# A gated delta rule on one core: filler products of the scan cut in halves, and each head's decays made one head earlier

## The reference, cut to what matters

```python
proj = h @ in_w                                        # q, k, v, z of every head, and a, b
qkv = silu(causal_dwconv(proj[..., :o1], conv_w))
q = l2norm(q) * (GDN_DK ** -0.5);  k = l2norm(k)
beta = sigmoid(b_in);  g = -exp(a_log) * softplus(a_in + dt_bias)
g = cumsum(g, axis=-1)                                 # inside a chunk
decay_mask = exp(where(causal, g[:, None] - g[None, :], -inf))
a_mat = where(strict, (k_beta @ k.T) * decay_mask, 0)
t_mat = inverse(eye + a_mat)
attn = where(causal, (q @ k.T) * decay_mask, 0)
...
def step(state, inp):                                  # the scan over chunks
    v_new = u_c - w_c @ state
    o_c = q_c @ state + attn_c @ v_new
    state = state * e_c + k_c.T @ v_new
o = rmsnorm(o) * silu(z);  out = o @ out_w
```

## Time and profile before

| what | value |
|---|---|
| median of 3 runs (lowest, highest) | 2101.68 us (2100.63, 2105.51) |
| the profiled execution's own time | 2100.75 us |
| its span, first to last instruction | 2098.8 us |
| PE busy, share of the span | 2047.3 us, 98% |
| DVE, ACT, POOL busy | 1351.1, 630.7, 244.7 us |
| mean granted TensorE clock | 0.997 |
| DeltaNet heads, from the first filler to the last o_flip | 458.4 to 1136.1 us of the span |

### The profile page before, as it was taken

One profiled execution on the slowest core, in us unless ns is written; L12 is line 12 of the kernel. 1 busy time (PEld: TensorE's weight loads), 2 busy tenths in 40 slices (PEclk: granted clock), 3 DMA queues, 4 the chain that ended last, 5 costly groups with the idle time before them and its releaser, 6 DMA issues. The chain is left out here.

```text
span 2098.8 us, 20772 instructions
## 1 busy us (share of the span) xinstructions
PE 2047.3 (98%) x6914; PEld 1044.5 (50%) x6914; DVE 1351.1 (64%) x1900; ACT 630.7 (30%) x1051; POOL 244.7 (12%) x188
## 2 busy tenths in 40 slices
PE   7999999999999999999998999999999999999998
PEld 4444444446566566656454454544444444444443
DVE  3787753266756656666823697439999997434633
ACT  4345531223443443443213410013211112241021
POOL 0000001113213213211102100011000000003200
PEclk9999999999999999999999999999999999999999
DMA  9333389241111211111420316389522222333021
GB/s 349 124 116 112 97 282 237 84 101 38 48 31 36 47 31 36 47 32 35 148 36 20 131 51 113 91 233 250 127 58 78 66 71 65 110 105 130 20 100 60
DMA packets 243824, 207.17 MB, mean 99 GB/s; under 512 B 52204, under 2 KB 202785, under 8 KB 243745
## 3 DMA queue, kind: packets, MB, share of 16 engines
q1 hardware_dynamic: 213393, 157.25, 25.1%
q0 software_dynamic: 13056, 42.99, 8.3%
q10 hardware_dynamic: 17312, 6.10, 1.3%
HBM read 182.55 MB, written 60.33 MB: 116 GB/s over the span
## 5 line engine op out<-in xcount | busy, mean ns | idle before, releaser
L2345 PE MATMUL bank<-hT,ring 128*128 128x512 f32 x576 | 254.2, 592 | 0.0
L2345 PE MATMUL bank<-resid,ring 128*128 128x512 f32 x432 | 191.3, 592 | 0.0
L2345 PEld LDWEIGHTS bank<-hT,ring 128*128 128x128 f32 x576 | 109.4, 190 | 137.8 <-issue 136.6
L1312 PE MATMUL bank<-hT,ring 128*128 128x512 f32 x336 | 157.7, 595 | 1.8 <-ACT silu_z L1549 1.8
L3265 DVE SCALAR_TENSOR_TENSOR yT<-s_arena,yT 128x1024 f32<-128x1024 f32 x120 | 152.8, 1273 | 0.0
L3265 DVE SCALAR_TENSOR_TENSOR s_arena<-s_arena 128x1024 f32<-128x1024 f32 x112 | 142.6, 1273 | 0.0
L2317 PE MATMUL bank<-hT,ring 128*128 128x512 f32 x320 | 139.4, 594 | 0.0
L2345 PEld LDWEIGHTS bank<-resid,ring 128*128 128x128 f32 x432 | 82.1, 190 | 103.3 <-issue 102.6
L2317 PEld LDWEIGHTS bank<-hT,ring 128*128 128x128 f32 x320 | 60.1, 190 | 73.7 <-issue 73.5
L2390 PE MATMUL bank<-ssm_y,ring 128*128 128x512 f32 x192 | 83.4, 592 | 0.0
L1312 PEld LDWEIGHTS bank<-hT,ring 128*128 128x128 f32 x336 | 58.4, 190 | 49.9 <-issue 49.5
(11 more groups left out here) (585 smaller groups left out, 3595.1 us busy)
## 6 DMA issues: line engine op xcount, KB each, us to landing
ada<-in_ada_w SPq DMA_DIRECT2D x8, 2048.0 KB, 8.1
ring<-in_gdn_in_w SPq DMA_DIRECT2D x32, 512.0 KB, 4.1
ring<-in_w_in SPq DMA_DIRECT2D x54, 256.0 KB, 2.9
ab_U_sums<-in_w_in POOLq DMA_DIRECT2D x6, 2048.0 KB, 19.2
resid<-in_x SPq DMA_DIRECT2D x8, 1024.0 KB, 8.8
ring<-in_lru_in_w SPq DMA_DIRECT2D x16, 512.0 KB, 3.9
ring<-ab_U_sums SPq DMA_DIRECT2D x32, 256.0 KB, 2.9
lru_arena<-in_ada_w SPq DMA_DIRECT2D x6, 1024.0 KB, 13.7
```

The costliest lines, as they stand in the source:

```text
L1312: last = nc.tensor.matmul(bank[:, to, :], w[:, k, :], v[:, k, :], start=(first and k == 0), stop=(k == KB - 1), skip_group_check=not only)
L2345: last = nc.tensor.matmul(bank[:, to, :], w[:, k, :], src[:, k, :], start=(start and k == 0), stop=(k == HK - 1), skip_group_check=not alone)
```

## The change

- The fillers from P4a on (the last six products) are cut into two matmuls of 256 columns each, so a filler is half as long there: 32 whole units and 48 halves.
- `fill` now puts 2 units instead of 4 ahead of `k_flip`, 12 instead of 13 behind `kk`, two halves (one unit before) ahead of the first state read, in each chunk two halves behind the read and two behind `new` (one unit each before), and, new, one half ahead of every state read from c=1 on. In the last head that place takes one whole unit. What is left stands behind the scan: 7 halves instead of 4 units, and in the last head 1 unit instead of 8.
- ACT's three copies in the scan move to c=2, c=3 and c=5.
- The decays of head h+1 are made in head h: the subtraction on DVE behind level 16, the mask on POOL behind the sums for half "b", the exponential on ACT at level 32 between `prod32` and `inv32`. Those of head 0 are made ahead of the loop: DVE behind the first convolutions, POOL behind its first weight sums, ACT behind the first silu(z).
- The query norm's root (`q_rms`) moves on ACT from level 32 to behind `prod64`, and its reciprocal on DVE (`q_inv`, `q_dec`) to behind `mem_zero`.

```diff
@@ project_pairs @@
-                        def product(pr, to, w, v, name, first=False, only=False):
-                            w = blocks(pr)[w]
+                        def product(pr, to, w, v, name, first=False, only=False, parts=1):
+                            w, width = blocks(pr)[w], HALF // parts
                             for k in range(KB):
...
+                                for n in range(parts):
+                                    cols_ = slice(n * width, (n + 1) * width)
+                                    last = nc.tensor.matmul(bank[:, to, cols_], w[:, k, :], v[:, k, cols_], start=(first and k == 0 and n == 0),
+                                                            stop=(k == KB - 1), skip_group_check=not only)
...
-                        yield from product("a", 0, "A22", tok_sum4, "P4")
+                        yield from product("a", 0, "A22", tok_sum4, "P4", parts=2)
...
-                        yield from product("b", 2, "S4", tok22, "P3")
+                        yield from product("b", 2, "S4", tok22, "P3", parts=2)
@@ body, tensor @@
-                        fill(4, 0)
+                        fill(2, 0)
...
-                        fill(13, 18)
+                        fill(12, 18)
...
                             if c == 0:
-                                fill(1, 0)
+                                fill(2, 0)
...
                             else:
+                                fill(1, 1)
                                 hd_dve.wait(pe, f"mem{c - 1}", h)
...
-                            fill(1, 2)
+                            fill(2, 2)
@@ body, gpsimd @@
+                    def masked(head):
+
+                        dve_r.wait(g, "rel", head)
+                        pool_r.mark(g.tensor_tensor(decayT[:, :, :], decayT[:, :, :], along(causal[:, :]), ALU.add), "rel")
+
                     def body(h, second, first):
-                        hd_dve.wait(g, "rel", h)
-                        hd_pool.mark(g.tensor_tensor(decayT[:, :, :], decayT[:, :, :], along(causal[:, :]), ALU.add), "rel")
...
                         if second:
                             weight_sums("b", h + 1)
+                            masked(h + 1)
...
                     weight_sums("a", 1)
+                    masked(0)
@@ body, scalar @@
+                    def decays(head):
+
+                        pool_r.wait(act, "rel", head)
+                        act_r.mark(act.activation(decayT[:, :, :], decayT[:, :, :], ACT.Exp), "decay")
...
-                        hd_pool.wait(act, "rel", h)
-                        hd_act.mark(act.activation(decayT[:, :, :], decayT[:, :, :], ACT.Exp), "decay")
...
-                            if s == levels[1]:
+                            if s == levels[1] and after is not None:
+                                decays(after)
+                            if s == levels[2]:
                                 hd_act.mark(act.activation(stat[:, 1, :], stat[:, 1, :], ACT.Sqrt, bias=eps2[:, 1:2], scale=float(P)), "q_rms")
...
-                            if c == 4 and after is not None:
+                            if c == 5 and after is not None:
                                 keep(2, "b", h, "P5", "C22")
...
                     take_z(0)
+                    decays(0)
                     for_heads(act, body)
@@ body, vector @@
+                    def relative(head):
+
+                        dve.wait_ge(g_in, (head + 1) * 16)
+                        dve_r.mark(dve.tensor_tensor(decayT[:, :, :], decayT[:, :, :], per_tok("g", head), ALU.subtract), "rel")
+
+                    relative(0)
...
-                        dve.wait_ge(g_in, (h + 1) * 16)
-                        hd_dve.mark(dve.tensor_tensor(decayT[:, :, :], decayT[:, :, :], per_tok("g", h), ALU.subtract), "rel")
...
+                            if n == 0 and after is not None:
+                                relative(after)
```

More of the change, by code:

```diff
@@ L1085, in block_program @@
                            + [f"vc{j}" for j in range(TAPS4)] + ["q_ss", "v_tok"]
-                           + [n for s in levels for n in halves(f"invT{s}") + (["q_inv", "q_dec"] if s == levels[1] else [])]
-                           + ["mem_zero"] + [f"{n}{c}" for c in range(NCH) for n in ("delta", "mem", "o")]
+                           + [n for s in levels for n in halves(f"invT{s}")]
+                           + ["mem_zero", "q_inv", "q_dec"] + [f"{n}{c}" for c in range(NCH) for n in ("delta", "mem", "o")]
                            + ["o_inv", "o_tok", "y"])
-            hd_pool = Steps(sem("gdn_pool"), ["rel"] + [f"part{s}" for s in levels[:-1]])
+            hd_pool = Steps(sem("gdn_pool"), [f"part{s}" for s in levels[:-1]])
+            dve_r, pool_r, act_r = Steps(sem("gdn_rel_dve"), ["rel"]), Steps(sem("gdn_rel_pool"), ["rel"]), Steps(sem("gdn_rel_act"), ["decay"])
             gdn_zero = sem("gdn_zero")
@@ L1536, in _ @@
                     act_q.ready(act)
+                    act_r.ready(act)
                     px_act.ready(act)
@@ L1624, in body @@
                                 output_square(h, c - 1)
-                            if c == 1 and after is not None:
+                            if c == 2 and after is not None:
                                 px_pe.wait(act, "P4a", h)
@@ L1628, in body @@
                                 px_act.mark(act.activation(padded[:, 1, PAD:PAD + HALF], bank[:, 0, :], ACT.Copy), "C21a")
-                            if c == 2 and after is not None:
+                            if c == 3 and after is not None:
                                 keep(1, "b", h, "P6", "C12")
-                            if c == 4 and after is not None:
+                            if c == 5 and after is not None:
                                 keep(2, "b", h, "P5", "C22")
@@ L1679, in _ @@
                     dve_q.ready(dve)
+                    dve_r.ready(dve)
                     dve_f.ready(dve)
@@ L1899, in body @@
                         hd_dve.mark(dve.memset(memory[:, 0, :], 0.0), "mem_zero")
+                        hd_act.wait(dve, "q_rms", h)
+                        hd_dve.mark(dve.reciprocal(stat[:, 1, :], stat[:, 1, :]), "q_inv")
+                        hd_dve.wait(dve, "q_inv", h)
+                        hd_dve.mark(dve.tensor_tensor(stat[:, 3, :], stat[:, 1, :], cols["exp_g"][:, h, :], ALU.mult), "q_dec")
                         for c in range(NCH):
```

32 lines of the change are left out of this document (13 added, 19 removed).

## The result

The changed kernel takes 2108.91 us (median of 6 runs, 2105.33 to 2110.62), the kernel before 2100.3 us in the same session (6 runs, 2098.83 to 2105.51). The ratio is 1.0033 with a 95% interval of 1.0022 to 1.0044: slower by a third of a percent. Forecast were 2101.0 us with a range of 2094.5 to 2106.5. The profiled execution of the changed kernel took 2110.62 us, its span is 2108.6 us.

The account below looks back on a forecast made before the run. PE, busy 98% of the span, bounds the kernel, with an equally long chain from AT to the inverse beside it. The terms summed to -0.1 us: 2100.7, or 2101.6 on the median's scale, given as 2101, range 2094.5 to 2106.5.

Parts of the forecast that it names:

- The fifth half: Scan's state reads: a half ahead of each removes the DVE wait and bare weight load, 0.37 us a read, -18.1 us.
- The copy: kept2b one chunk later: PE waits 0.6 us a head at chunk 6's first P3b, +4.2 us.
- Behind the scan: Seven halves cover o_tok's path before o_flip barely: 0.1 us lost in each of seven heads, +0.7 us.
- The load at `k_sq`: Heads 1 to 6: ACT's table load ahead of k_sq delays AT; PE waits 1.15 us a head, +6.9 us.
- rival 1: ACT's table load does not count, heads 1 to 6 lose nothing: 2093.8 us; chance 0.20.
- The decays in the inverse: At level 32, ACT's load and exponential for the next head stay hidden: cost nothing, cover 0.1 us thin.
- rival 3: DVE's subtraction and POOL's last sum delay each other, decays late in the inverse: 2103.8 us; chance 0.10.
- Rival 4: Every table load of the loop costs about twice the row's time: another 9.7 us, 2110.4 us; chance 0.02.
- Rival 2: The state reads' weight load stays bare, up to 0.11 us at 49 reads: +5.4, 2106.1 us; chance 0.13.
- The last head, "-0.8": Last head: output-weight wait -1.2, reads -1.9, but one unit left to cover o_tok +2.3; together -0.8 us.
- Head 0, "+5.9": Head 0: mask, exponential and load ahead of k_sq delay the transposes 3.3 us, three fewer fillers 2.6: +5.9 us.
- Reads and halves, "-18.1" and "+1.1": Scan reads save 0.37 us each over 49, -18.1 us; 24 more products a head from halving cost +1.1 us.

Follow-up runs that it names:

- e3: The change plus one tiny silu behind head 0's exponential, so the loop's first activation needs no table load: 2100.36 us, ratio to before 0.9988.
- e7: The change with products, fillers and copies as in the kernel before, so the decays part alone: 2104.09 us, ratio to before 1.0002.
- e12: The decays part alone, plus the small silu ahead of the loop and head 0's mask ahead of the weight sums: 2101.61 us, ratio to before 0.9997.
- e8: The change without the last head's units ahead of the state reads, so eight units stand behind its scan again: 2106.59 us, ratio to before 1.0013.
- e11: The kernel before with one unit ahead of each state read from c=1 on, in the last head alone: 2104.28 us, ratio to before 1.0013.
- e5: The change with POOL making head 0's mask ahead of head 1's first weight sums, not behind: 2098.79 us, ratio to before 0.9982.
- e4: The change with ACT's copy kept2b put back from chunk 5 to chunk 4: 2102.36 us, ratio to before 1.0003.
- e1: The kernel before, run again without any edit: 2102.45 us, ratio to before 1.0002.
- e10: The change with silu ahead of the loop, kept2b in chunk 4, head 0's mask first and the last head's reads without units: 2085.89 us, ratio to before 0.9921.
- e6: The kernel before with the filler part alone (halves, fifth half, later copies), decays where they were: 2108.88 us, ratio to before 1.0026.
- e2: The changed kernel, run again without any edit: 2109.85 us, ratio to before 1.0037.

## Why the prediction was wrong

**Right.** The fifth half: the wait for DVE's update and the bare weight load are gone, and a chunk of 3.27 us was forecast at 3.26. From first to last read a head without the copy's wait takes 23.01 us and holds seven more halves than the 22.23 us of before; with 0.43 us for each half that is 22.23 + 3.03 - 23.01 = 2.25 us won, 0.32 a read, where the sum had 0.37 less some 0.02 for the halves. The copy: 0.52 us of wait and 0.65 a head were forecast at 0.6. Behind the scan a head loses 0.03 us ahead of o_flip, where 0.1 was forecast. The load at `k_sq`: 1.15 us a head forecast, 1.34 to 1.37 measured by e3; the forecast start of `k_sq` and arrival of PE (35.54 us, against 32.95 + 2.65 = 35.60 in e3) were right, and rival 1 is excluded. The decays in the inverse cost nothing: POOL's last sum took 2.16 us instead of 1.28 beside DVE's subtraction (POOL and ACT, change, level 32), yet the exponential ended 0.17 us before PE released the copy behind it.

```profile
659.79 2.16 POOL L1257 TENSOR_TENSOR gate_b<-ring,yT 128x512 f32<-128x512 f32 x1
661.90 2.36 POOL L1262 TENSOR_TENSOR decayT<-decayT,causal 128x1024 f32<-128x1024 f32 x1
...
664.82 1.06 ACT L1584 ACTIVATE decayT<-decayT 128x1024 f32<-128x1024 f32 x1
666.05 1.08 ACT L1630 ACTIVATE buf_b<-bank 128x512 f32<-128x512 f32 x2 [0.17 <-PE bank L1454]
```

So rival 3's contention is there, 0.9 us of it, and the slack takes it up. Rival 4 is excluded: `k_sq` begins 0.01 us after the load, and e3 gives 1.37 us a load, not 2.7. The Trainium skill ("ScalarE: Activation LUTs", section What ACT_TABLE_LOAD costs) puts draining on top of the 1.28 us; no row here shows it. Rival 2 (a bare weight load at the reads) is excluded by the 0.22 us from read to filler.

**Wrong, by the steps of the sum.** The sum prices each new wait of PE by its length and puts what the clock does behind the wait at nothing. That failed at two terms (1 and 2); two more were mis-sized (3 and 4).
1. *The last head, "-0.8".* The step that failed with the wrong sign. Its parts were sized rightly (-1.1 for the wait for the output weights by e7 and e12, forecast -1.2; 2.15 us of wait at o_flip against 2.3; reads and o_flip together +0.5 by the change against e8, forecast -1.9 + 2.3 = +0.4), but the step ended at o_flip. The wait is followed by a slower clock in the next block's products, and e11 prices this edit alone at +2.5 us (interval 0.4 to 5.0) against the +0.4 of the sum, so that the term comes to about +1.3.
2. *Head 0, "+5.9".* The chain was right. From the first filler to the end of AT passed 16.0 us, as forecast (474.3 - 458.4 = 15.9); to the transposes 42.9 us, where 42.1 were forecast: the products behind the wait ran at half clock (3.62 us instead of 1.95), which the sum did not have. Head 0 lost 5.1 us net, 0.9 more than the sum's parts for it (5.9, less the reads' 2.6, and 0.9 for halves, copy and o_flip). e5 gains 8 because PE's own road, with next to nothing to wait for, is shorter still than I took it: 35.1 us from the first filler to the first transposes, where 42.1 - 5.9 = 36.2 was reckoned. That the mask could stand ahead of the sums at no cost wasn't seen.
3. *Reads and halves, "-18.1" and "+1.1".* Measured 0.32 us a read net of the halves, not 0.35; some 1.5 us over 49 reads.
4. *The load, "+6.9".* Mis-sized by 0.2 us a head, some 1.2 us.

By the profiles the heads come to +3.0 instead of -0.1, and what follows the uncovered wait adds about 2 (2.5 - 0.4): 2100.75 + 5 = 2106, on the scale of the medians 2107. Measured were 2108.9 and 2109.85.

**Open.** The last 2 to 3 us. Taken one by one, the edits of e3, e4, e5 and e8 gain 10, 7, 11 and 4.6 us against the change (from the ratios), 33 together; all four at once gain 24 (0.9921 against 1.0035, the mean of the change's two ratios). From the heads alone the first three come to 8, 4 and 8. So every single edit seems to take away some 2 to 3 us besides its own, which is at the edge of the intervals (each about 0.0012, 2.5 us). The profiles show stretches at half clock elsewhere, some 30 and 410 us after the start, near 1170 and near 1290 us; they are there in some profiles of one and the same kernel and not in others, the kernel before among them. Two profiles of each kernel can't settle whether the change has more of these, but the mean granted clock of every run is on record, too. It is 0.9966 in the mean of 87 runs of the kernel before (sessions of e1 to e12) and 0.9936 in the mean of 11 runs of the change. Counted as (1 - clock) times the span, half clock takes 7.2 us of the one and 13.4 us of the other: 6.2 us more, an upper estimate, since PE also waits in some of these stretches. Head 0's stretch (6.8 us at half speed, 3.4 lost) and the 6.5 us more behind the last o_flip (some 3 lost) make up about as much. So lost clock can be the greater part of what the change lost, and there is no sign that it has many more such stretches elsewhere. The other kernels fit the places named above: e3 and e4, which take out short waits, leave the count as it is (14.1 and 13.0 us); e5 (9.2) and e8 (10.5), which take out the two long waits, lower it; e11 raises that of before to 10.7, and e10 comes back to 7.5.

One place has a longer wait too, and no experiment touched it. Near 1290 us PE waits for the transfer of `u_scratch`: 5.75 and 5.47 us in the two profiles of the change, 3.06 and 3.32 in those of before, 1.9 to 5.7 in the others. Timeline of PE, change, then before:

```profile
1291.47 5.00 PE L2439 MATMUL bank<-yT,s_arena 128*64 128x128 f32 x64 [5.75 <-DMA yT<-u_scratch]
```

```profile
1283.02 3.71 PE L2416 MATMUL bank<-yT,s_arena 128*64 128x128 f32 x64 [3.06 <-issue]
```

These 2.4 us are as much as is open; whether the change causes them is not shown.

## What to carry to other kernels

Where PE's own road and a chain beside it are equally long, shorten both: each part of this change alone gained nothing (the decays even with their losses out, the fillers with theirs in), both with their losses out gained 16 us. When an activation is moved to the end of a preparation, look at which table it leaves for the loop: one small activation of the other function behind it saved a load in every pass. And price a wait of TensorE not only by its length: look at the clock granted to the work behind it, also across the border of the stage that is changed.

## What the runs showed of the hardware

- Where TensorE waited for head 0's inverse (2.67 us in e6, 5.4 to 6.5 us in the change, e2, e3, e4 and e8), the 16 products behind the wait took 3.42 to 3.78 us; where it didn't wait there, in the other kernels, 1.95 or 2.05 us. Behind the last o_flip's wait of 2.15 us the next block's products were slower in eight of eight profiles (8.5 to 10.2 us instead of 7.10); without it in two of six (8.8 us). Behind the wait of 2.14 to 2.15 us at the last head's first filler the products were slower in three of four; where that wait was 1.01 us, in none of ten.
- Two products of 256 columns cost hardly more than one of 512: seven halves took 3.05 us from the first to o_flip (619.17 to 622.22 in head 2 of the change), 0.436 each with some 0.03 us ahead of o_flip in it, where 0.86 / 2 = 0.43 is a straight half.
- A POOL sum beside a DVE instruction with both inputs in SBUF, the engines' working memory, looked like one that waits for DVE to end. A sum of 128x512 takes 1.27 us alone. The first one in head 0 (e5, 456.71) took 3.34 us while DVE formed a sum of 128x2048 (456.63 to 458.92), and one in the inverse of head 2 (change, 659.79) took 2.16 us beside the decays' subtraction (659.44 to 660.79): both ended 1.1 to 1.2 us after DVE did. Beside DVE instructions with one input in PSUM (the `v_tok` and `invT` rows at 657.11 and 658.24 of the same head) the sums kept 1.27 and 1.28 us.
